# Context visits spaced wider through the first block and x's mixer, in a two-block kernel on one core

## What is computed

```python
q = (hc @ w_query).reshape(PEER_CHUNK, PEER_HEADS, 2, D_KEY // 2)
s = jnp.einsum('chpd,hpnd->chpn', q, sub_keys)
s_top, i_top = lax.top_k(s, PEER_TOPK)                 # 16 of 128, twice per head
...                                                    # 256 sums, 16 best of them: eid, gate
u = jnp.take(u_tab, eid, axis=0)
act = jax.nn.gelu(jnp.einsum('chkd,cd->chk', u, hc)) * gate
v = jnp.take(v_tab, eid, axis=0)
return jnp.einsum('chk,chkd->cd', act, v)
```

## Time and profile before

| what | value |
|---|---|
| median of 3 runs | 3821.81 us (3816.61 to 3829.53) |
| the profiled execution | 3827.01 us |
| its span | 3825.3 us |
| TensorE matmul busy | 2651.7 us, 69% |
| VectorE busy | 1810.1 us, 47% |
| GpSimd busy | 1481.5 us, 39% |
| bytes moved | 1047.09 MB, mean 274 GB/s |

### The profile page before, as it was taken

How to read it: one execution, slowest core, us unless ns; L and a number is a source line. 1 busy time by engine, 2 the same in 40 slices (tenths; PEclk the granted TensorE clock), 3 DMA queues, 4 the chain that set the end, 5 groups by cost and what they waited for, 6 DMA issues and landing times.

```text
span 3825.3 us, 35082 instructions
## 1 busy us (share of the span) xinstructions
PE 2651.7 (69%) x11672; PEld 1361.5 (36%) x11672; DVE 1810.1 (47%) x4395; ACT 502.2 (13%) x1117; POOL 1481.5 (39%) x1577
## 2 busy tenths in 40 slices
PE   4899747989999888885565555457788455555555
PEld 3367513456666534674121000004377400000000
DVE  1521586443333577217774444443711795444444
ACT  1220101320100124001020000002210100000000
POOL 0000045443444443200555666661000066666665
PEclk8899857899999988997667666668699766666666
DMA  7668469878999985631789999993023089999998
GB/s 255 229 224 317 178 233 333 319 285 324 348 352 352 335 289 199 218 139 46 285 324 338 356 359 359 363 358 139 33 94 121 29 325 361 361 360 355 360 361 331
DMA packets 325906, 1047.09 MB, mean 274 GB/s; under 512 B 27424, under 2 KB 38752, under 8 KB 325728
## 3 DMA queue, kind: packets, MB, share of 16 engines
q0 software_dynamic: 240192, 880.90, 62.1%
q1 hardware_dynamic: 85536, 163.95, 12.3%
HBM read 1043.70 MB, written 1.05 MB: 273 GB/s over the span
## 4 chain that ended last, share of the span: by engine, by line
PE 38%; DVE 22%; issue 13%; another core or an unknown queue 12%; DMA 5%; PEld 4%; ACT 2%; PEldq 2%; SPq 1%; ACTq 0%; DVEq 0%; POOL 0%; POOLq 0%
PE ps L378 18%; DVE UV L953 8%; PE ps L401 5%; PE ps L416 5%; PEld ps L378 4%; DMA W<-in_w_in 3%; PE ps L370 3%; DVE arena L1191 2%; PEldq L365 2%; PE ps L503 1%; DVE arena L1290 1%; DVE arena L1296 1%; DVE arena L1287 1%; PE ps L680 1%
## 5 line engine op out<-in xcount | busy, mean ns | idle before, releaser
L953 DVE SCALAR_TENSOR_TENSOR UV<-ps,UV 128x1024 f32<-128x1024 f32 x768 | 913.3, 1222 | 1045.3 <-remote 561.0
L1905 POOL DMA_INDIRECT UV<-in_u_tab,idxT x768 | 725.1, 944 | 1530.0 <-DVEq L1364 766.0
L401 PE MATMUL ps<-hs,selb 96*128 96x512 bf16 x1536 | 586.0, 494 | 700.4 <-DVE UV L953 375.8
L1915 POOL DMA_INDIRECT UV<-in_v_tab,idxT x768 | 723.8, 943 | 418.3 <-issue 206.9
L378 PE MATMUL ps<-H,W 128*128 128x256 f32 (+2 forms) x3296 | 684.0, 370 | 73.7 <-DMA W<-in_w_in 45.8
L378 PEld LDWEIGHTS ps<-H,W 128*128 128x128 f32 (+1 forms) x3296 | 587.4, 199 | 184.6 <-issue 58.3
L401 PEld LDWEIGHTS ps<-hs,selb 96*128 96x128 bf16 x1536 | 122.7, 108 | 1279.9 <-DVE UV L953 713.2
L416 PE MATMUL ps<-UV,acts 128*32 128x512 f32 x3072 | 538.4, 781 | 36.6 <-issue 24.8
L378 PE MATMUL ps<-arena,W 128*128 128x256 f32 (+1 forms) x1632 | 370.9, 385 | 21.6 <-issue 11.1
L378 PEld LDWEIGHTS ps<-arena,W 128*128 128x128 f32 (+1 forms) x1632 | 304.9, 190 | 107.4 <-issue 62.6
L1502 ACT ACTIVATE arena<-ps 128x512 f32<-128x512 f32 (+7 forms) x310 | 167.5, 550 | 999.5 <-PE ps L378 783.3
(11 more groups left out here) (154 smaller groups left out, 1771.9 us busy)
## 6 DMA issues: line engine op xcount, KB each, us to landing
W<-in_w_in SPq DMA_DIRECT2D x30, 2048.0 KB
UV<-in_w_mod POOLq DMA_DIRECT2D x24, 2048.0 KB, 14.1
W<-in_w_ff SPq DMA_DIRECT2D x16, 2048.0 KB
UV<-in_w_ada POOLq DMA_DIRECT2D x12, 2048.0 KB, 11.9
W<-in_w_out SPq DMA_DIRECT2D x8, 2048.0 KB
W<-in_w_query SPq DMA_DIRECT2D x6, 2048.0 KB
UV<-in_u_tab,idxT POOLq DMA_INDIRECT x768
UV<-in_v_tab,idxT POOLq DMA_INDIRECT x768
```

What stands on the lines that cost most here:

```text
L401: last = mm(ps[:, HB + 2 * (tok % 2) + hf, :], one, hs[:, n % 2, t // GROUP, hf * 512:(hf + 1) * 512], start=True, stop=True)
L953: dve.scalar_tensor_tensor(out=Us[:, j, :], in0=ps[:, b:b + 2, :].rearrange("p a b -> p (a b)"), scalar=1.0, in1=Us[:, j, :], op0=MUL, op1 ...
L1905: pool.indirect_dma_start(Us[:, j, :], None, A["u_tab"], off).then_inc(sem(f"u_arrived{j}"), 16)
L1915: pool.indirect_dma_start(Vs[:, j, :], None, A["v_tab"], off).then_inc(sem(f"v_arrived{j}"), 16)
```

## The change

The budget per visit becomes a variable. It is 6.6 us at first (the context's second routing), 8.8 us through the first block and x's mixer, and 6.6 us again from there on. VectorE, ScalarE and GpSimd follow the lists that TensorE's program makes, so nothing else is edited.

```diff
-PACE = 6.6
+PACE, PACE_LATER = 6.6, 8.8
...
             streaming, seen, ready, owed = [False], [0], [0], [0.0]
+            pace = [PACE]
...
                 owed[0] += us
-                while owed[0] >= PACE and seen[0] < min(segment[1], PAIRS * ready[0]):
-                    owed[0] -= PACE
+                while owed[0] >= pace[0] and seen[0] < min(segment[1], PAIRS * ready[0]):
+                    owed[0] -= pace[0]
                     visit(seen[0])
                     visits_at[key].append(seen[0])
                     seen[0] += 1
-                owed[0] = min(owed[0], PACE)
+                owed[0] = min(owed[0], pace[0])
...
             open_stream(0)
             route_second("c0")
+            pace[0] = PACE_LATER
             first_block()
             mixer("x0")
+            pace[0] = PACE
             stream("tile 0 done", max(seen[0], PAIRS + 2))
             route_first("x0")
             stream("tile 1 done", max(seen[0], 2 * PAIRS + 2))
```

## The result

The changed kernel takes 3838.84 us (median of 7 runs, 3833.39 to 3845.33), the kernel before 3822.57 us in the runs beside it (7 runs, 3816.61 to 3834.87). The ratio is 1.0044, with a 95% interval of 1.0029 to 1.0058: slower by 11 to 22 us. The forecast was 3842, slower.

A forecast was written before the change was run, and what follows sets the result against it. No engine was near full over the whole, so stages were priced separately, TensorE setting the feed-forward and VectorE x0's first routing. Terms -45.6, +12 and +54 sum to +20, carried to the median 3821.8 as 3842 us; range 3812 to 3864.

The forecast's parts named there:

- First block: From f's norm through the feed-forward and last norm: 19 visits fewer, 45.6 us saved.
- Feed-forward: First block's feed-forward, TensorE busy 294 of 301 us: 34 visits become 26, 2.25 us each, 18 us saved.
- x0's mixer: x0's front, attention, merge, out and norm: 3 visits more in all, 12 us more.
- The front: Front of x0's mixer: 19 visits become 14, 2.2 us each, 11 us saved.
- The window: x's hidden, queries, scores and first routing: 16 visits more, 54 us more.
- The query part: Window up to VectorE's first top-sixteen: six visits, uncovered queries and the last visit's two dots, 30 us more.
- the steps: Tile 2's routing on VectorE, 59.0 us before: ten visits at 2.41 us each, 24 us more.
- the uncovered queries: Next tile's two queries, hidden under VectorE's routing before: the routing now waits for them, 15.1 us more.
- rival (A): Whole kernel: the forecast, slower; moved visits gain nothing and queries lose their cover; 3830 to 3856 us, chance 0.52.
- Rival (B): First block held by transfers: 19 visits fewer give back 114 us, net -48, 3774 us; chance 0.12.
- Rival (C): Window cheaper, queries partly absorbed, first block saving 3 us a visit: sum 0, 3822 us; chance 0.24.
- Rival (D): Merges: weight loads at half rate beside gathers in every pair, +49 us, 3871 us at full price; chance 0.12.

The follow-up runs named there:

- the doubling: Tile 3's two query halves computed twice, in the changed kernel (3871.18 us) and in the kernel before (3815.89 us), one run each.
- the run that gives the cover back: Changed kernel without visits behind the next tile's queries or tile 2's first three steps, beat 9.4 behind the other nine: 0.9995 of the kernel before.
- the first try: Changed kernel with no visit behind the next tile's two query halves in x's first routing: 3841.32 us, 1.005 of the kernel before.
- pace 7.4: Budget per visit 7.4 us in place of the changed kernel's 8.8, leaving no visit for the window: 3833.55 us, 1.0033 of the kernel before.

## Why the prediction was right

Step by step, forecast and then measured. **First block**: 45.6 saved; 51.6. Feed-forward 18 and 19.1, norm and in1 6.2 and 8.9, attention 7.0 and 7.7, merge, out and norm 14.4 and 15.9. Each term was right in kind, and the savings came out 6 to 44% above it. For the feed-forward the runs show why. Its mean visit cost 2.0, not the 2.25 of the prediction, whose visit-free base of 225 was 8 us too short; but the last eight, the ones that left, cost 2.4. The two errors nearly cancel, and that part of the agreement is luck. The agreement in f's attention is partly luck too: the 3.5 a visit was borrowed from x0's, and up to 5 us lie between repeats of this stage. **x0's mixer**: 12 more; 8.0 more. The front gave 17.6 instead of 11, again because the visits that left were the dear ones (3.5 for each of the five, while the mean is 2.2); the attention gave 4.7 instead of 7, the other way (2.4 for each that left, 4.0 for each that stayed, over x1's 39.0); the merge and out product took 27.6 where 26 were forecast, the norm 2.7 instead of 4. **The window**: 54; 56.5. The query part 30 and 32.8, the steps 24 and 23.7. Sum: +20 forecast, +13 by the stages, +16.3 by the medians. The window, where the forecast's argument lies, was right to 2.5 us; ahead of it the visits were priced by their mean and the sum came out 10 us too slow.

The term that carries the most of argument, the uncovered queries, is shown by the doubling in both kernels and by the run that gives the cover back. The rest of rival (A), that the moved visits otherwise cancel, is shown by that same run's ratio of 0.9995. Rival (B), the transfers, falls with the first block without visits. Rival (C) had a part of it: the saving in the first block was 2.7 a visit, between the forecast's 2.4 and its 3, but nothing of the queries was absorbed. Rival (D), weights at half rate beside gathers in every pair, would have put x0's merge at 140 + 74 = 214 us; it took 187.5, with 185 forecast. The Trainium skill ("DMA: Bandwidth & Descriptors", section "Queues, rings and completion order") says that each DMA engine goes round-robin between the queue rows with work; the half rate throughout that the prediction worked out from it is not what these traces show. The direction is right: a visit in the merge and out product costs 3.2 us at 8 visits and 3.3 at 16, the surplus over 2.1 is TensorE's wait for weights, and taking visits out of the merge is what made a faster kernel.

The order of events in the profile came as announced. Two times are off: x0's front was reached 55 us sooner rather than 46 (1238.2), and 4 of those lie ahead of the first block; and tile 2's first dot came at 1837.25 rather than near 1848, since the stages ahead of it were shorter by that much.

## What to carry to other kernels

A hole in which DMA and TensorE idle isn't free room if a third engine fills it: here a visit cost 2.4 to 2.5 us in a window that VectorE sets, and 1.9 to 2.4 in the feed-forward, which TensorE sets. Before work is put into such a window, look in each in-order program for what was hidden under the bounding engine; one dot placed behind 15 us of queries pulled them all onto the path, and moving that dot one step on only moved the wait. And price a filler where it stands: here the gain lay not in spacing the visits but in keeping them out of the stage whose weight loads they delay.

## What was not expected

The price of a visit isn't constant within a stage. In the feed-forward it is 1.9 us up to 26 visits and 2.4 for the next eight; in x0's front 1.8 each for the first 14 (161.3 against the 136.5 us of x1's) and 3.5 for the next five. In f's attention it is 1.6 and then 3.9 by these profiles, but the clock of the visit-free run and the up to 5 us between repeats make both numbers uncertain. x0's merge with its out product doesn't follow: 27.6 us for the visits from 8 to 16, and next to nothing for three more, whose run waits 34.5 us for weights where the changed kernel waits 37.1. How much of that is due to their places among the chunks was not separated.

Stages with the same program differ more between executions than the change is worth. The stretch from the c1 front's norm to x1's, with 109 visits at some 350 GB/s, took 654.4 us in the kernel before and 655.1 in the changed kernel, so it has no part in their difference, but 645.8 in the first try and 661.5 in the run without visits in x0's merge. Here are the changed kernel's and the first try's:

```profile
1970.90:2626.00 655.10, 363.43 (x1427) 72.42 (x1427) 294.58 (x605) 48.93 (x150) 399.77 (x425) 0.68 0.93 348
...
1980.10:2625.90 645.80, 360.02 (x1427) 68.06 (x1427) 293.97 (x605) 48.84 (x150) 398.69 (x425) 0.68 0.94 353
```

The steps without visits, which VectorE sets, repeat to 0.1 us (59.0 in the kernel before and at pace 7.4), and the feed-forward with 26 visits, which TensorE sets, to 1.5 us in six profiles. Small changes are better read in such stages than from totals.
